# Gate and up projections of a one-core model block: seven block products for eight, with the block sums made on VectorE

## The reference, cut to what matters

```
h2 = rmsnorm(h_res, norm2_w[l])
gu = h2 @ w_gate_up[l]                                  # 1024 -> 2 * 2816
h_res = h_res + (jax.nn.silu(gu[..., :D_FF]) * gu[..., D_FF:]) @ w_down[l]
```

## Time and profile before

| | us |
|---|---|
| median of 3 runs | 1650.03 (1648.68 to 1650.18) |
| span of the profiled execution | 1648.4 |
| PE busy in it | 1622.5 (98%) |
| DVE, ACT, POOL busy in it | 822.6, 699.7, 904.8 |

### The profile page before, as it was taken

The page is one execution under the profiler, slowest core; times in us unless marked ns, Lnnn a source line. Parts: engine busy times, 40 slices in busy tenths (PEclk is TensorE's granted clock), DMA queues, the critical chain, the costliest instruction groups (busy, mean ns, idle before and its releaser), DMA issues.

```text
span 1648.4 us, 23603 instructions
## 1 busy us (share of the span) xinstructions
PE 1622.5 (98%) x9465; PEld 1396.5 (85%) x9465; DVE 822.6 (50%) x1329; ACT 699.7 (42%) x1048; POOL 904.8 (55%) x515
## 2 busy tenths in 40 slices
PE   7999989999999999999999999999999999999998
PEld 7999988899998888888888888888888888888887
DVE  7778955735343001131212122128999972457744
ACT  6666554333233222243223333236543553366652
POOL 3455645333446445545555554458978665456661
PEclk9999989999999999999999999999999999999999
DMA  5586388564323243332233333333332422333332
GB/s 205 156 262 188 89 259 266 148 197 151 127 73 101 89 144 100 102 98 94 91 101 95 97 102 102 103 102 93 99 101 91 128 90 90 93 100 102 102 100 80
DMA packets 122357, 202.47 MB, mean 123 GB/s; under 512 B 32624, under 2 KB 73736, under 8 KB 122248
## 3 DMA queue, kind: packets, MB, share of 16 engines
q1 hardware_dynamic: 119912, 197.46, 38.4%
q10 hardware_dynamic: 2336, 3.51, 0.6%
HBM read 170.97 MB, written 29.97 MB: 122 GB/s over the span
## 4 chain that ended last, share of the span: by engine, by line
PE 88%; DVE 8%; ACT 1%; issue 1%; POOL 1%; DMA 0%; SPq 0%; DVEq 0%; ACTq 0%
PE ps L435 76%; PE ps L1928 3%; DVE cacc L2424 3%; DVE inv L667 1%; DVE prd L664 1%; PE ps L975 1%; PE ps L989 1%; PE ps L983 1%; PE ps L996 1%; PE ps L1000 1%; POOL hp L2790 1%; PE ps L942 1%; PE ps L961 1%; DMA x_in<-in_x 0%; PE ps L1898 0%
## 5 line engine op out<-in xcount | busy, mean ns | idle before, releaser
L423 POOL TENSOR_TENSOR w_lo<-w_raw,w_hi 128x1024 fp32r<-128x1024 f32 x264 | 633.5, 2408 | 422.9 <-ACT w_hi L417 410.5
L435 PE MATMUL ps<-hp,w_hi 128*128 128x512 f32 (+2 forms) x2432 | 595.0, 344 | 0.0
L435 PEld LDWEIGHTS ps<-hp,w_hi 128*128 128x128 f32 x2432 | 402.0, 189 | 53.3 <-issue 2.1
L435 PE MATMUL ps<-hp,w_lo 128*128 128x512 f32 (+2 forms) x1216 | 370.6, 342 | 0.0
L417 ACT ACTIVATE w_hi<-w_raw 128x1024 fp32r<-128x1024 f32 x264 | 277.2, 1053 | 136.7 <-DMA w_raw<-in_w 129.0
L435 PEld LDWEIGHTS ps<-hp,w_lo 128*128 128x128 f32 x1216 | 210.9, 189 | 26.2
L435 PE MATMUL ps<-n_hi,w_hi 128*128 128x512 f32 x464 | 180.7, 389 | 0.0
L435 PE MATMUL ps<-n_hi,w_lo 128*128 128x512 f32 x464 | 180.5, 389 | 0.0
L435 PE MATMUL ps<-n_lo,w_hi 128*128 128x512 f32 x464 | 180.5, 389 | 0.0
L1358 DVE SCALAR_TENSOR_TENSOR ps<-u_in,par,ps 128x511 f32<-128x511 f32 (+14 forms) x210 | 154.6, 739 | 6.5
L435 PEld LDWEIGHTS ps<-n_hi,w_lo 128*128 128x128 f32 x464 | 87.1, 188 | 18.2
(11 more groups left out here) (434 smaller groups left out, 2609.0 us busy)
## 6 DMA issues: line engine op xcount, KB each, us to landing
w_raw<-in_w SPq DMA_DIRECT2D x264, 512.0 KB, 3.5
d_y<-zero SPq DMA_DIRECT2D x6, 688.0 KB, 6.0
d_x<-zero SPq DMA_DIRECT2D x6, 688.0 KB, 6.2
d_at<-at SPq DMA_DIRECT2D x16, 256.0 KB, 3.2
d_kc<-kc SPq DMA_DIRECT2D x16, 256.0 KB, 3.3
d_qd<-eg SPq DMA_DIRECT2D x16, 256.0 KB, 3.2
d_p<-dec SPq DMA_DIRECT2D x16, 256.0 KB, 3.4
AT<-d_at SPq DMA_DIRECT2D x16, 256.0 KB, 6.6
```

Of the source, the lines that this page charges most:

```text
L423: e.tensor_tensor(w_lo[:, u % RAW, :], w_raw[:, u % RAW, :], w_hi[:, u % RAW, :].bitcast(F32), ALU.subtract).then_inc(s_lo, 1)
L435: mm = e.matmul(ov, w, r[:, k, t0:t1], start=(first and n == 0 and p3 == 0), stop=(last and n == len(tiles) - 1 and p3 == 2))
```

## The change

The gate and up weights leave the unit stream and come in 88 **quarters** (GN; 4 for each of the 22 tiles) from an array of their own. A quarter holds four 128x128 blocks: gate and up, each for two blocks of 128 input features. With the tokens in two halves of 256 this is a product of 2x2 blocks by 2x2 blocks, eight block products. The change makes it with seven, from sums of weight blocks and sums of token blocks (`GPROD` lists weight, token block, PSUM bank and half of each product), each in three matmuls of 128x256: 21 matmuls for a quarter, 84 for a tile.

- The four sum blocks of the token side are made once for each quarter of the features, in "out" (`dve_rows`, `act_rows`, `dve_rows_lo`).
- The three instructions of `sum_quarter` make the four sum blocks of a quarter on DVE, from SBUF to SBUF, each waiting for the one before; ACT copies 128x896 to the high part (`round_quarter`, three buffers), POOL subtracts 128x896 (`split_quarter`, six buffers).
- `dve_joined` adds up the four sums in PSUM in four parts, with a `sum_quarter` ahead of each part. POOL no longer makes the remainder of the product; DVE does (part 3). Only the gate is scaled by 1/rms; the factor for up is applied to the result of "down", one more 128x512 instruction on DVE for each of its 8 tiles.
- The first two "down" units are rounded by ACT inside tile 21, after its copy of bank 0; from "down" on the ring buffers are used in another order (`lies`).

```diff
-         ("out", KT), ("gu", 2 * FT), ("down", 3 * KT), ("glu", 2 * KT), ("bval", KT), ("agate", KT), ("pool", 4),
+         ("out", KT), ("down", 3 * KT), ("glu", 2 * KT), ("bval", KT), ("agate", KT), ("pool", 4),
...
+GN = 4 * FT
+GRAW, GHI = 6, 3
+GW = 7 * P
+HALVES = 256
+GPROD = [(2, 1, 1, 0), (0, 4, 1, 1), (4, 5, 3, 0), (6, 2, 3, 1), (3, 6, 2, 0), (5, 3, 2, 1), (1, 0, 0, 0)]
...
+        def load_quarter(e, n):
+            if n >= GRAW:
+                e.wait_ge(*pg.at("quarter", n - GRAW + 1))
+            elif n:
+                e.wait_ge(s_pe, BASE["out"] + min(RAW + n, KT))
+            e.dma_start(g_raw[n % GRAW][:, 0:4, :], a["wg"][n].rearrange("p (t m) -> p t m", m=P)).then_inc(s_quarter[n % GRAW][0], 16)
+        def sum_quarter(e, n):
+            if n < GN:
+                r = g_raw[n % GRAW]
+                e.wait_ge(s_quarter[n % GRAW][0], s_quarter[n % GRAW][1] + 16 * (n // GRAW + 1))
+                e.tensor_tensor(r[:, 4:6, :], r[:, 0:1, :].to_broadcast([P, 2, P]), r[:, 1:4:2, :], ALU.add).then_inc(dg.sem, 1)
+                e.wait_ge(*dg.at("quarter", 3 * n + 1))
+                e.tensor_tensor(r[:, 0, :], r[:, 5, :], r[:, 1, :], ALU.add).then_inc(dg.sem, 1)
+                e.wait_ge(*dg.at("quarter", 3 * n + 2))
+                e.tensor_tensor(r[:, 6, :], r[:, 0, :], r[:, 2, :], ALU.add).then_inc(dg.sem, 1)
+        def round_quarter(e, n):
+            if n < GN:
+                e.wait_ge(*dg.at("quarter", 3 * n + 3))
+                if n >= GHI:
+                    e.wait_ge(*pg.at("quarter", n - GHI + 1))
+                else:
+                    e.wait_ge(s_pe, BASE["out"] + RAW + 1 + n)
+                e.activation(g_hi[n % GHI][:], g_raw[n % GRAW][:], ACT.Copy).then_inc(ga.sem, 1)
+        def split_quarter(e, n):
+            if n < GN:
+                e.wait_ge(*ga.at("quarter", n + 1))
+                e.tensor_tensor(g_lo[n % GRAW][:], g_raw[n % GRAW][:], g_hi[n % GHI][:].bitcast(F32), ALU.subtract).then_inc(pz.sem, 1)
+        def pe_quarter(e, n):
+            j, t = divmod(n, 4)
+            b0 = 4 * (j % 2)
+            e.wait_ge(*pz.at("quarter", n + 1))
+            if j == 0:
+                e.wait_ge(*hh.at("n2", 3 * t + 3))
+            for w, b, bank, half in GPROD:
+                first = t == 0 and half == 0
+                if first and j == 0:
+                    e.wait_ge(*dv.at("out", 5 + bank))
+                if first and j == 1 and bank == 1:
+                    e.wait_ge(*rt.at("n2", 2))
+                if first and j >= 1 and bank == 0:
+                    e.wait_ge(*ev.at("gu", 2 * j - 1))
+                if first and j >= 2 and bank == 1:
+                    e.wait_ge(*ev.at("gu", 2 * j - 2))
+                if first and j >= 2 and bank == 2:
+                    e.wait_ge(*dv.at("gu", 2 * j - 2))
+                wh, wl = g_hi[n % GHI][:, w, :], g_lo[n % GRAW][:, w, :]
+                bh, bl = hi_block(t, b), b_lo[t][:, b, :]
+                for p3, (l, r) in enumerate(((wh, bh), (wh, bl), (wl, bh))):
+                    mm = e.matmul(ps[:, b0 + bank if bank else 0, HALVES * half:HALVES * half + HALVES], l, r,
+                                  start=first and p3 == 0, stop=t == 3 and p3 == 2 and (half == 1 or bank == 0))
+            mm.then_inc(pg.sem, 1)
+        def halves(v):
+            return v.rearrange("p (b n) -> p b n", b=2)
+        def both(v):
+            return v.unsqueeze(1).to_broadcast([P, 2, HALVES])
+        def dve_rows(e, j):
+            t, n = j // 2, pcol("norm2", j)
+            e.wait_ge(*dv.at("out", j + 1))
+            r = b_raw[t]
+            if j % 2 == 0:
+                e.tensor_scalar(r[:, 0:4:3, :], halves(x[:, j, :]), n, None, ALU.mult).then_inc(fd.sem, 1)
+            else:
+                e.tensor_scalar(r[:, 1:3, :], halves(x[:, j, :]), n, None, ALU.mult).then_inc(fd.sem, 1)
+                e.wait_ge(*fd.at("n2", 6 * t + 1 + 1))
+                e.tensor_tensor(r[:, 5, :], r[:, 2, :], r[:, 3, :], ALU.subtract).then_inc(fd.sem, 1)
+                e.tensor_tensor(r[:, 3, :], r[:, 0, :], r[:, 3, :], ALU.subtract).then_inc(fd.sem, 1)
+                e.wait_ge(*fd.at("n2", 6 * t + 3 + 1))
+                e.scalar_tensor_tensor(r[:, 4, :], r[:, 3, :], -1.0, r[:, 2, :], ALU.mult, ALU.subtract).then_inc(fd.sem, 1)
+                e.wait_ge(*fd.at("n2", 6 * t + 4 + 1))
+                e.scalar_tensor_tensor(r[:, 6, :], r[:, 4, :], -1.0, r[:, 1, :], ALU.mult, ALU.subtract).then_inc(fd.sem, 1)
+        def act_rows(e, j):
+            t = j // 2
+            for i in ((0,), (1, 2))[j % 2]:
+                e.wait_ge(*fd.at("n2", 6 * t + (0, 1, 5)[i] + 1))
+                e.activation(hi_piece(t, i), b_raw[t][:, PIECES[i], :], ACT.Copy).then_inc(hi.sem, 1)
+        def dve_rows_lo(e, t):
+            e.wait_ge(*fd.at("n2", 6 * t + 5 + 1))
+            for i in range(3):
+                e.wait_ge(*hi.at("n2", 3 * t + i + 1))
+                e.tensor_tensor(b_lo[t][:, PIECES[i], :], b_raw[t][:, PIECES[i], :], hi_piece(t, i).bitcast(F32), ALU.subtract).then_inc(hh.sem, 1)
+        def dve_joined(e, j, part):
+            b0, gate, mid = 4 * (j % 2), row(j % 2), row(2 + j % 2)
+            left, up = ps[:, b0 + 1, :], ps[:, b0 + 2, :]
+            n = 6 * j
+            if part == 0:
+                e.wait_ge(*ev.at("gu", 2 * j + 1))
+                e.tensor_tensor(mid[:, HALVES:], mid[:, 0:HALVES], left[:, HALVES:], ALU.add).then_inc(fd.sem, 1)
+                e.tensor_tensor(left[:, 0:HALVES], mid[:, 0:HALVES], left[:, 0:HALVES], ALU.add).then_inc(fd.sem, 1)
+                e.wait_ge(*fd.at("gu", n + 1))
+                far = ps[:, b0 + 2:b0 + 4, :].rearrange("p b n -> p (b n)")[:, HALVES:3 * HALVES]
+                e.tensor_tensor(halves(gate), both(mid[:, HALVES:]), halves(far), ALU.add).then_inc(fd.sem, 1)
+            if part == 1:
+                e.wait_ge(*fd.at("gu", n + 3))
+                e.tensor_tensor(left[:, HALVES:], gate[:, 0:HALVES], ps[:, b0 + 3, HALVES:], ALU.add).then_inc(fd.sem, 1)
+                e.tensor_tensor(halves(up), both(gate[:, HALVES:]), halves(up), ALU.add).then_inc(fd.sem, 1)
+                e.wait_ge(*fd.at("gu", n + 4))
+                if j == 0:
+                    e.wait_ge(*rt.at("n2", 2))
+                e.tensor_tensor(left, left, row(4), ALU.mult).then_inc(fd.sem, 1)
+            if part == 2:
+                e.wait_ge(*fd.at("gu", n + 5))
+                e.wait_ge(*ev.at("gu", 2 * j + 2))
+                e.scalar_tensor_tensor(up, up, -1.0, gate, ALU.mult, ALU.mult).then_inc(dv.sem, 1)
+            if part == 3:
+                e.wait_ge(*hi.at("gu", j + 1))
+                e.tensor_tensor(y_lo[:, j, :], up, y_hi[:, j, :].bitcast(F32), ALU.subtract).then_inc(dv.sem, 1)
...
+            for n in range(GN):
+                pe_quarter(e, n)
+                if n == 1:
                     e.wait_ge(*ad.at("out", KT - 1))
...
+                    pe_cols(e, row(4), 0, 6).then_inc(ss.sem, 1)
+                if n == 2:
                     e.wait_ge(*rc.at("n2", 1))
...
+                    pe_spread(e, 7, 16).then_inc(tb_.sem, 1)
+            e.wait_ge(*dv.at("gu", 2 * FT - 2))
...
+                if j < KT - 2:
+                    round_unit(e, BASE["out"] + j + 2)
+                if j == KT - 2:
+                    round_quarter(e, 0)
+                if j == KT - 1:
+                    round_quarter(e, 1)
+                    round_quarter(e, 2)
                 e.wait_ge(*dv.at("out", j + 1))
...
                 if j >= 3:
                     e.wait_ge(*ad.at("out", j - 2))
                 e.activation(row(4) if j == 0 else row(2 + j % 2), x[:, j, :], ACT.Square).then_inc(sq.sem, 1)
+                act_rows(e, j)
+            round_quarter(e, 3)
             e.wait_ge(*ss.at("n2", 1))
...
+            e.activation(small[:, 16:20], ps[:, 6, 0:4], ACT.Sqrt, bias=eps_col).then_inc(rt.sem, 1)
+            round_quarter(e, 4)
             e.wait_ge(*tb_.at("n2", 1))
...
+            e.activation(row(4), ps[:, 7, :], ACT.Copy).then_inc(rt.sem, 1)
+            round_quarter(e, 5)
+            for j in range(FT):
+                e.wait_ge(*pg.at("quarter", 4 * j + 4))
+                e.activation(row(2 + j % 2, HALVES), ps[:, 0, 0:HALVES], ACT.Copy).then_inc(ev.sem, 1)
+                round_quarter(e, 4 * j + 6)
+                round_quarter(e, 4 * j + 7)
+                if j == FT - 1:
+                    round_unit(e, BASE["down"])
+                    round_unit(e, BASE["down"] + 1)
+                e.wait_ge(*fd.at("gu", 6 * j + 6))
+                e.activation(row(j % 2), ps[:, 4 * (j % 2) + 1, :], ACT.Silu).then_inc(ev.sem, 1)
+                round_quarter(e, 4 * j + 8)
+                round_quarter(e, 4 * j + 9)
+                e.wait_ge(*dv.at("gu", 2 * j + 1))
+                e.activation(y_hi[:, j, :], ps[:, 4 * (j % 2) + 2, :], ACT.Copy).then_inc(hi.sem, 1)
...
+            for j in range(KT):
```

(54 more changed lines are left out.)

128 lines of the change are left out of this document (44 added, 84 removed).

## The result

The changed kernel takes 1750.6 us (median of 4 runs, 1747.9 to 1752.6) against 1650.1: the ratio is 1.061, 95% interval 1.059 to 1.062. The forecast was 1759. The profiled execution took 1752.6 us, with a span of 1750.8.

The account below looks back on a forecast made before the run. PE bounded the kernel before; afterwards SBUF ports shared by DVE and POOL would. Stage 22 x 15.6 - 5 + 3.9 + 6 = 348, less 239.4: +109 us; span 1648.4 becomes 1757, plus 1.6: 1759 us, range 1675 to 1835.

Parts of the forecast that it names:

- PE's rate: Gate and up stage: a 128x256 matmul takes 0.1197 us, a tile 10.06 instead of 10.88, saving 18.0 us over 22 tiles.
- Exclusion at the ports: DVE additions with two SBUF inputs and POOL's remainders lock each other out; at least 10.8 us a tile.
- The order of events within a tile: Gate and up stage: DVE's additions wait for POOL's remainders 1.9 + 1.8 + 1.8 + 1.6 = 7.1 us; a tile takes 15.6.
- the ring through DVE, ACT and POOL: Each quarter must pass DVE, ACT and POOL in turn, and DVE stands at its next addition while POOL splits.
- DVE's own work: Per tile, quarter additions 4.3 us and joins of the PSUM sums 4.5, together 8.8 us.
- First tiles: Start of the gate and up stage: the first two tiles run partly on quarters prepared in "out", 5 us less.
- The wait for the last residual: End of "out": PE's third product of quarter 0 waits for DVE, between 0.5 and 12 us, taken as 6.
- The pause ahead of "down": PE idles while the first "down" unit is copied for, rounded and split (0.4, 1.05, 2.4): 3.9 us more.
- PE's waits in the stage: Gate and up stage: PE idle before matmuls for some 5 us a tile, released by POOL's remainder.
- 1: Gate and up stage: no real exclusion for these operands, PE binds, 1637 us, faster; chance 12%.
- 2: Gate and up stage: ports bind but engines interleave well, 10.8 to 13 us a tile, 1655 to 1705 us; chance 15%.
- 3: Gate and up stage: PE's clock falls as well, 18.8 to 20 us a tile, 1830 to 1855 us; chance 13%.

Follow-up runs that it names:

- x2_psum_operand: Changed kernel with the second input of the three weight-block additions taken from an idle PSUM bank, sums not the reference's: 1645.4 us, ratio 0.996 to the kernel before.
- x3_half_splits: Changed kernel with each of POOL's quarter remainders made in two instructions of 448 columns instead of one of 896: 1709.2 us, ratio 1.034 to the kernel before.
- x4_pairs: Changed kernel with DVE making the additions of two quarters together, in step: 1684.7 us, ratio 1.019 to the kernel before.

## Why the prediction was right

**PE's rate.** Forecast 0.1197 us a matmul of 128x256 and 10.06 a tile. Measured in x2_psum_operand, where PE runs unhindered: 0.1194 and 10.03. Right.

**Exclusion at the ports.** Forecast from three collisions in the trace of before, as the Trainium skill's "SBUF — State Buffer", section "SBUF: two separate sides", has it. The tile shown above repeats them, and x2_psum_operand against the changed kernel proves it: 105 us (106 by the ratios) for the place of one operand.

**The order of events within a tile.** Forecast: four waits, 7.1 us together, a tile of 15.6. Measured: four waits, 7.2, a tile of 15.16. Counted from the moment that the gate is ready (L618 ends at 892.76), POOL ends its two remainders in a row at 5.99 us (5.9 forecast) and the third at 9.38 (9.35); the fourth, read from the tile before, comes at 12.7 (12.95). Which additions meet POOL differs in part: I had two first additions and two second ones, and it is one first, one second and two third ones. L514 at 894.26 got through because it began 0.06 us before POOL's remainder at 894.32, and the two behind it waited in its place. The count and the ring through DVE, ACT and POOL are as forecast.

The term that was mis-sized is DVE's own work: 8.8 us forecast, 15.16 - 7.2 = 7.9 measured (4.0 instead of 4.5 for the joins, 3.9 instead of 4.3 for the additions). The forecast's two accounts of the tile did not agree either, since 8.8 + 7.1 is 15.9 and not 15.6. The tile came out 0.4 us too large, 9.7 us over 22 tiles, which is more than the difference between 1759 and 1751; the small terms below take some of it back, and so the total is closer than its largest term. x3_half_splits and x4_pairs were drawn by the same working and came out 16 and 5 us lower than drawn; the working errs to the slow side each time.

**The small terms.** First tiles -5: the stage is 338.6 us, less 22 x 15.16, 6.4, 3.9 and 1.7 of column matmuls and spreading, gives -6.9. The wait for the last residual: 6 forecast, 6.4 measured. The pause ahead of "down": 3.9 and 3.89. Behind that pause PE lost 1.9 us at the slow clock, which the sum did not have. PE's waits in the stage were forecast at some 5 us a tile and are 3.0: PE ran slowly for part of the time in which it had been drawn idle. The 3.0 us ahead of the stage are no effect of the change that can be shown.

**Rivals.** 1 is refuted by x2_psum_operand, though its number (1637) is near what that kernel took (1645). 2 came nearest in x4_pairs, where the order helps, and its lower bound of 10.8 was never reached with the additions' inputs in SBUF; the changed kernel's 15.16 lies above its 13. 3: the clock did fall, to 0.88 in the stage. For the 1848 matmuls of the windows PE needs 220.7 us at 0.1194 each and was busy for 259.4, so some 39 us of the stage were lost to slow running. They did not lengthen it, and two tiles of the changed kernel show this side by side (windows, columns as in the earlier trace rows):

```profile
827.84:842.96 15.12, 12.22 (x79) 11.80 (x78) 14.85 (x22) 4.94 (x7) 8.69 (x5) 0.77 0.22 60
1009.53:1024.68 15.15, 10.54 (x86) 10.13 (x86) 14.88 (x21) 4.94 (x7) 8.71 (x5) 1.00 0.26 70
```

At a clock of 0.77 and at 1.00 a tile is equally long, and DVE is busy for all but 0.3 us of both. Of the 16 tiles from 812.70 to 1054.93 us one is at 1.00 and the others lie between 0.77 and 0.97, and every one lasts 15.12 to 15.16 us. By the rule of the Trainium skill's "TensorE: Matmul & The Clock Gate", section "HAM oscillation — how this bites in real kernels", that the prediction cites, pauses between bursts bring the clock down each time: the trace agrees for most tiles but not for all, since the one from 1009.53 has a pause of 3.4 us and stays at 1.00. A tile of 18.8 us did not follow.

## What to carry to other kernels

Before moving work to an engine with idle time, look at where its operands lie, not only at its busy share: a VectorE instruction with two SBUF inputs and GpSimd's take turns, whole instruction by whole instruction. Add up both engines' time at the ports for one turn of the loop, and if the sum nears the loop's length, bring one operand from PSUM. Where instructions of that kind can't be avoided, put them where the other engine is idle, so that fewer of them meet it (x4_pairs: two waits a tile instead of four), and keep the other engine's instructions short (x3_half_splits).

## What was not expected

- Halving POOL's instruction gained 41 us, though it gave POOL more to do: two halves are 2.5 us (1.24 each on average, with some waiting), one whole is 2.19.
- A fall of the clock to 0.88 and 39 us of slow running did not show in the time, as the two tiles above show.
- POOL gets the ports between two additions that do not depend on each other, too (x4_pairs at 854.15).
- The seven products, freed of the ports, win 1642.8 against 1651.5 us: 9 of the 18.7 us that PE saves (22 tiles of 10.88 less 10.03). Most of the rest is lost at the start: 6.4 us of waiting, and behind it PE takes 6.6 us for 36 matmuls that need 4.3, at a clock of 0.50 from 746 to 750 us. At the end and within the stage it waits for another 0.9.
